# Modulation vectors on four column groups of 32 with 256-wide pieces instead of two of 64, and ten convolution taps moved into the attention heads

## What is computed

```python
def modulation(cvec, w_mod_l, b_mod_l):
    m = jax.nn.silu(cvec) @ w_mod_l + b_mod_l          # w_mod_l: 1024 x 6144
    return m.reshape(cvec.shape[0], 6, D_MODEL)

def trunk_layer(x, mod, ...):
    sh1, sc1, g1, sh2, sc2, g2 = [mod[:, i][:, None, :] for i in range(6)]
    h = rms_norm(x, n1) * (1.0 + sc1) + sh1
    q, k, v, u = jnp.split(h @ w_in, ...)
    # QK-norm; rotary positions for latent tokens
    attn = block_attention(q, k_all, v_all)            # 8 heads of 64, 2 key heads
    conv = conv_module(u, dw_w, dw_b, ln_g, ln_b)      # gate, 31 taps depthwise, layer norm, silu
    x = x + g1 * (jnp.concatenate([attn, conv], axis=-1) @ w_out)
    h2 = rms_norm(x, n2) * (1.0 + sc2) + sh2
    x = x + g2 * grouped_moe(h2, ...)                  # 16 experts, top 2 of one group
    return x, k, v
```

## Time and profile before

| | |
|---|---|
| median of 3 runs | 1130.35 us |
| all three | 1130.08, 1130.35, 1140.29 us |
| profiled execution | 1134.84 us, of which the span 1133.0 us |
| granted TensorE clock, mean | 0.938 of full |
| TensorE busy (products) | 1003.9 us, 89% |
| VectorE, ScalarE, GpSimd busy | 393.6, 152.3, 116.3 us |
| moved by DMA | 329.83 MB, mean 291 GB/s |

### The profile page before, as it was taken

How to read it: one execution, slowest core, us unless ns; L and a number is a source line. 1 busy time by engine, 2 the same in 40 slices (tenths; PEclk the granted TensorE clock), 3 DMA queues, 4 the chain that set the end, 5 groups by cost and what they waited for, 6 DMA issues and landing times. The chain is left out here.

```text
span 1133.0 us, 11425 instructions
## 1 busy us (share of the span) xinstructions
PE 1003.9 (89%) x4328; PEld 471.3 (42%) x4328; DVE 393.6 (35%) x857; ACT 152.3 (13%) x357; POOL 116.3 (10%) x176
## 2 busy tenths in 40 slices
PE   4799999999799998899899989999788888987993
PEld 1555544545233333333366534555433333333331
DVE  0159954334411111111035996434511111111106
ACT  1100144220000000000020014422000000000001
POOL 0100400501000000000111020050100000000001
PEclk9899989998899999999899999999689899999897
DMA  9926991259999996999980375235966999999814
GB/s 341 354 117 238 291 366 70 95 189 360 419 404 423 425 372 273 413 422 424 360 306 24 149 277 215 75 115 195 371 237 240 417 422 425 424 423 422 353 28 167
DMA packets 64406, 329.83 MB, mean 291 GB/s; under 512 B 6992, under 2 KB 9680, under 8 KB 47924
## 3 DMA queue, kind: packets, MB, share of 16 engines
q1 hardware_dynamic: 44224, 277.89, 61.2%
q0 software_dynamic: 8496, 28.68, 6.9%
q10 hardware_dynamic: 11588, 21.95, 5.9%
HBM read 306.67 MB, written 21.82 MB: 290 GB/s over the span
## 5 line engine op out<-in xcount | busy, mean ns | idle before, releaser
L1746 PE MATMUL ps<-big 128*64 128x512 f32 x1024 | 245.5, 631 | 29.0 <-DMA big<-in_w_up_dram 11.8
L1762 PE MATMUL ps<-big,scr 128*64 128x512 f32 x624 | 151.0, 623 | 5.3 <-DVE scr L1399 4.3
L1441 PE MATMUL ps<-big 128*128 128x384 f32 (+2 forms) x448 | 147.9, 492 | 5.2 <-ACT big L777 5.2
L1746 PEld LDWEIGHTS ps<-big 128*64 128x64 f32 x1024 | 81.7, 145 | 168.1 <-issue 157.1
L1102 DVE SCALAR_TENSOR_TENSOR scr<-scr,convw 128x384 f32<-128x384 f32 x240 | 134.0, 611 | 2.3
L1410 DVE TENSOR_TENSOR scr<-ps,scr 128x256 f32<-128x256 f32 x32 | 13.6, 425 | 315.5 <-ACT scr L932 315.5
L1441 PEld LDWEIGHTS ps<-big 128*128 128x128 f32 x448 | 86.0, 193 | 64.7 <-issue 24.6
L1457 PE MATMUL ps<-big,cs_rep 128*64 128x512 f32 x320 | 80.8, 656 | 14.0 <-DMA big<-in_w_mod_dram 14.0
L1762 PEld LDWEIGHTS ps<-big,scr 128*64 128x64 f32 x624 | 51.2, 143 | 91.1 <-issue 89.0
L1662 PE MATMUL ps<-big 128*128 128x512 f32 x192 | 84.4, 594 | 1.4 <-ACT big L817 1.4
L1746 PE MATMUL ps<-big,scr 128*64 128x512 f32 x224 | 51.3, 612 | 5.9 <-DVE scr L1388 5.9
(11 more groups left out here) (220 smaller groups left out, 819.7 us busy)
## 6 DMA issues: line engine op xcount, KB each, us to landing
big<-in_w_gate_dram SPq DMA_DIRECT2D x32, 2048.0 KB, 15.8
big<-in_w_up_dram SPq DMA_DIRECT2D x32, 2048.0 KB, 19.7
big<-in_w_down_dram SPq DMA_DIRECT2D x32, 2048.0 KB, 16.7
big<-in_w_mod_dram SPq DMA_DIRECT2D x23, 2048.0 KB, 15.5
big<-in_w_in_dram SPq DMA_DIRECT2D x6, 2048.0 KB, 26.8
expert_rows<-scr ACTq DMA_DIRECT2D x74, 128.0 KB, 8.2
big<-in_w_out_dram SPq DMA_DIRECT2D x4, 2048.0 KB, 15.6
expert_rows<-x ACTq DMA_DIRECT2D x1, 6912.0 KB, 42.0
```

The costliest lines, as they stand in the source:

```text
L1441: mm = pe.matmul(out, stationary(k), moving(k), start=(k == 0), stop=(k == n - 1))
L1746: mm = pe.matmul(ps[b * TT:(b + 1) * TT, bank, :].rearrange("p (m n) -> p m n", m=2), tokens(k), w[:, :, k, b * HF:(b + 1) * HF], start=(k ...
L1762: mm = pe.matmul(ps[b * TT:(b + 1) * TT, bank, :], src[:, k % 2 * P + k // 2 * TT:k % 2 * P + (k // 2 + 1) * TT], w[:, k, b * SEG:(b + 1) ...
```

## The change

`LANES` goes from 2 to 4. With it `LW` goes from 512 to 256 and `LP` from 64 to 32. A vector becomes 8 x 4 products of 32 x 256. The column products of a vector become 8 x 4 instead of 8 x 2, each with 32 columns of weights. `lane_in` and `lane_out` issue four DMAs instead of two each time, each over half the partitions (or the same two rows) and half as wide. `mod_take` handles 256 columns instead of 512. The expected semaphore counts follow. `rowC` is now the first 256 columns of `sg`. The tap constants go from 80, 6, 6, 4, 4 to 80, 6, 0, 0, 5: the 6 taps between rope(0) and rope(1) and the 4 behind mod_take(2) are taken away in each layer, and the heads take 26 instead of 16.

```diff
--- before.py
+++ after.py
@@ -34,7 +34,7 @@
 NT = CAP // TT
 HF = FF // 2
 SEG = 512
-LANES = 2
+LANES = 4
 LW = D // LANES
 LP = P // LANES
 SLOTS = 6
@@ -124,7 +124,7 @@
 for first_, n0, more_ in ((0, 16, 15), (1, 15, 16), (2, 16, 15)):
     CONV_ORDER += [p for n in range(more_) for p in ((first_, n0 + n), (first_ + 1, n))]
 CONV_ORDER += [(3, n) for n in range(15, TAPS)]
-EARLY_TAPS, ROPE_TAPS, BETWEEN_TAPS, LATE_TAPS, HEAD_TAPS = 80, 6, 6, 4, 4
+EARLY_TAPS, ROPE_TAPS, BETWEEN_TAPS, LATE_TAPS, HEAD_TAPS = 80, 6, 0, 0, 5
 assert sorted(CONV_ORDER) == [(m, n) for m in range(CM) for n in range(TAPS)]
 
 
@@ -286,12 +286,13 @@
         kT = cut(512)
         acc = cut(CM * CAP).rearrange("p (m n) -> p m n", m=CM)
         zT = cut(CM * CONV_W).rearrange("p (m n) -> p m n", m=CM)
-        assert o >= 5120 + 3 * LW
+        assert o >= 6656
 
         qk_sq = scr[:, TILES * 640 + 2 * 640:2 * TILES * 640 + 2 * 640].rearrange("p (t n) -> p t n", t=TILES)
         vall = cut(4 * KVW).rearrange("p (c n) -> p c n", c=4)
         ck = cut(KVW)
-        sg = rowC = cut(CH)
+        sg = cut(CH)
+        rowC = sg[:, 0:LW]
         assert o <= 9832
         hT_all = big[:, at_hT:at_hT + TILES * D].rearrange("p (j k n) -> p j k n", j=TILES, k=KD)
         gate_sig = [h[:, m, CH:CH + CAP] for m in range(3)] + [h[:, 2, 0:CAP]]
@@ -595,7 +596,7 @@
 
                 pool.wait_ge(mod_taken, taken_at(l, 2))
                 lane_out(pool, mod_dram[:, 2 * D:3 * D], rowC, modC_st)
-                pool.wait_ge(modC_st, (l + 1) * 32)
+                pool.wait_ge(modC_st, (l + 1) * LANES * 16)
                 spread(gateB[:, :, :], 2, bcG_in)
 
                 pool.wait_ge(slot_used[slot_of(("in", l, 3))], uses(("in", l, 3)))
@@ -626,7 +627,7 @@
                     if t:
                         ln_silu(t - 1)
                 ln_silu(2)
-                pool.wait_ge(modB_st, l * 48 + 48)
+                pool.wait_ge(modB_st, (l + 1) * (LANES + 1) * 16)
                 spread(scaleB[:, :, :], 4, bcA_in)
                 spread(shiftB[:, :, :], 3, bcA_in)
 
@@ -651,7 +652,7 @@
 
                 pool.wait_ge(mod_taken, taken_at(l, 5))
                 lane_out(pool, mod_dram[:, 5 * D:6 * D], rowG, modG_st)
-                pool.wait_ge(modG_st, (l + 1) * 32)
+                pool.wait_ge(modG_st, (l + 1) * LANES * 16)
                 spread(gateB[:, :, :], 5, bcG_in)
                 for e in range(E):
                     def run(t):
@@ -961,22 +962,22 @@
 
                 bank = mod_bank(l, c)
                 if c == 2:
-                    dve.wait_ge(rowC_in, (l + 1) * 32)
+                    dve.wait_ge(rowC_in, (l + 1) * LANES * 16)
                 if c == 3:
-                    dve.wait_ge(rowB_in, (l + 1) * 48)
+                    dve.wait_ge(rowB_in, (l + 1) * (LANES + 1) * 16)
                 if c == 5:
-                    dve.wait_ge(rowG_in, (l + 1) * 32)
+                    dve.wait_ge(rowG_in, (l + 1) * LANES * 16)
                 if c == 8:
                     dve.wait_ge(mod_half_ps, l + 1)
                 else:
                     n = pieces(l, min(c, 4 if c == 9 else c))[-1][0]
                     dve.wait_ge(slot_used[slot_of(n)], uses(n))
                 if c < 2:
-                    v.tensor_copy(rowA[:, c * LW:(c + 1) * LW], ps[:, bank, :]).then_inc(mod_taken, 1)
+                    v.tensor_copy(rowA[:, c * LW:(c + 1) * LW], ps[:, bank, 0:LW]).then_inc(mod_taken, 1)
                     return
                 if c < 8:
-                    row = (rowC[:, :], rowB, None, rowG)[c - 2]
-                    v.tensor_tensor(row, ps[:, bank, :], row, ALU.add).then_inc(mod_taken, 1)
+                    row = (rowC, rowB, None, rowG)[c - 2]
+                    v.tensor_tensor(row, ps[:, bank, 0:LW], row, ALU.add).then_inc(mod_taken, 1)
                 else:
                     half = slice(c % 2 * SEG, (c % 2 + 1) * SEG)
                     row, gain = rowS[:, half], gainB[:, half]
@@ -1454,7 +1455,7 @@
                             loaded(n)
                         w = slot_k(slot_of(n), b - a)[:, k - a, :]
                         for lane in range(LANES):
-                            mm = pe.matmul(ps[lane * LP:(lane + 1) * LP, mod_bank(l, j), :], cs_rep[:, k, :],
+                            mm = pe.matmul(ps[lane * LP:(lane + 1) * LP, mod_bank(l, j), 0:LW], cs_rep[:, k, :],
                                            w[:, lane * LW:(lane + 1) * LW], start=(k == 0), stop=(k == KD - 1))
                         if k == b - 1:
                             mm.then_inc(slot_used[slot_of(n)], 1)
```

## The result

The changed kernel takes 1125.53 us (median of 20 runs, 1119.47 to 1132.13), the kernel before, timed beside it, 1131.41 (20 runs, 1127.87 to 1140.29). The ratio is 0.9945, with a 95% interval of 0.9924 to 0.9966: 6 us faster, where 17.9 were forecast. 1125.53 is above the range's end of 1125. The profiled execution of the changed kernel has 1125.83 us, against 1134.84 of before.

A forecast was written before the change was run, and what follows sets the result against it. Outside the experts engine waits bind, inside them often the weights' stream. 4.0 + 4.2 + 3.3 + 0.7 + 4.6 + 2.7 - 1.6 = 17.9 us: profiled 1134.84 to 1117.0, median forecast 1112.5, range 1106 to 1125.

The forecast's parts named there:

- The pace: TensorE's vector rows: four column groups run side by side, 54 ns a record; column products 26 to 28 ns.
- Rivals 1 to 3: Records: (1) 59 to 65 ns, 1119.8 us, 10%; (2) two groups together, 1127, 8%; (3) groups in turn, 1175, 5%.
- Start and attention: Shorter vectors, copies and columns, and moved taps: gain 4.0 us at the start, 4.2 in layer 0's attention, 4.6 in layer 1's.
- The heads: Attention heads: the added taps hide in VectorE's idle time while TensorE runs without a gap; no change.
- rival 4: Pace comes, part given back through VectorE, GpSimd, the stream or lower clock in waits: 12 to 6 us left, 17%.
- Routing: Ahead of the experts: layer 0's expert 0 starts 5.7 us earlier, layer 1 gains 2.7; gather moves with slot_tok.
- The experts' stream: Layer 0's experts: weights for expert 4 land late, so only 3.3 of 5.7 us pass; in layer 1 all passes.
- The column products of layer 1: Alone on TensorE ahead of expert 15: 128 rows at 27 ns against 64 at 61, gain 0.7 us.
- The stores ahead of layer norm: Before the output projection, GpSimd issues two stores more: loss 0.8 us in each layer, 1.6 together.

The follow-up runs named there:

- dma_late: Changed kernel with GpSimd's four gate-bias issues moved behind the three rope roots; 1123.7 us, 0.9936.
- cols_split: Changed kernel with layer 1's column products in two places, vector 0's in another bank and one expert earlier; 1121.8 us, 0.9921.
- before_fill_more: Kernel before with unused extra products: 11 rounds before layer 1's last rope, 5 and 16 in the gather waits; 1126.31 us, 0.9947.
- fill_gather: Changed kernel with unused extra products in the two gather waits alone, 14 rounds in layer 0, 18 in layer 1; 1125.56 us, 0.9947.

## Why the prediction went wrong, by its own steps

**The pace (right).** 56 ns a row of the vectors and 18 of the column products, 54 and 27 forecast. Rivals 1 to 3 are out. So is the reading by which matmuls would be decoded at about 62 ns each, from TensorE: Matmul & The Clock Gate of the Trainium skill: four rows start within 20 ns and a fifth 216 ns behind the first, and column products take 18 ns a row, ends taken in, or 36 a product of two rows. The same page of the Trainium skill has a floor of about 25 ns from start to start: rows went under it here, whole products did not. Its three column groups at 2.38 times one are not met either; four ran at 54 ns, four times one.

**Start and attention (right).** Start: from vector (0,1)'s beginning to the projection 15.1 us before and 10.5 after, 4.6 gained where 4.0 stood. Layer 0: VectorE's second add follows the vectors' beginning by 13.7 us instead of 16.7, 3.0 gained where 4.2 stood. Most of the missing 1.2 is the last vector rows: 1.94 us at the lower level, 1.07 at the upper, behind a wait of 2.35 us, which the working had made possible and not counted. GpSimd's roots came late as said, if less: VectorE's first add stands 1.9 us earlier where 1.5 was reckoned, so that the roots cost 1.3 of the 3.25 us and not 1.8. VectorE's timeline after:

```profile
112.41 0.83 DVE L1121 TENSOR_TENSOR scr<-scr,stat 128x640 f32<-128x640 f32 x1 [0.83 <-POOL stat L585]
...
119.14 0.82 DVE L1121 TENSOR_TENSOR scr<-scr,stat 128x640 f32<-128x640 f32 x1 [0.83 <-POOL stat L585]
...
135.69 0.42 DVE L980 TENSOR_TENSOR big<-ps,big 128x256 f32<-128x256 f32 x1 [3.05 <-PE ps L1458]
```

Layer 1: 4.1 where 4.6 stood. Of the pair's gain at the start 2.9 us are neither: the transposes of x (L1495) begin at 25.1 us instead of 28.0 since the first loads landed earlier in that execution.

**The heads (a term put at nothing).** "So nothing" was argued from VectorE's cover and held at the upper level: heads are 6.68 us apart in all kernels. But the heads' length is set by the clock in their first 20 us, and that differs from one execution to the next; extra products in the wait ahead of them shorten the low stretch and don't make it sure to be gone. The working named this in rival 4, which it gave 17%, and counted the vectors' saving in layer 1 as worth nothing. Against the one profile of before the heads lost 2.4 us in layer 0 and 5.1 in layer 1 over three profiles; over all profiles, as said above, it is under 2 us that can be put down to the change.

**Routing (the gather taken as fixed).** Layer 0 should have won 4.9 us up to expert 0 and won 2.4 (2.5 in the pair). Up to the last router products 1.45 were lost, where 0.8 stood: the stores' 0.6, and router rows at the lower level (3.33 us for 16 instead of 1.96). slot_tok was 3.8 us earlier behind them, as forecast (4.05), and the rows behind the transposes saved 1.6 (1.7). But the gather gave 1.4 back, which no step had: the sum let it follow its issue at the old distance. Layer 1's 1.9 did not come at all: slot_tok gained 1.8 instead of 2.7, the gather took 9.3 us instead of 8.0 behind its issue, and TensorE's wait grew to 9.80, with the lower level through the products around it.

```profile
815.35 1.95 PE L1731 MATMUL ps<-table_sb,scr 128*128 128x128 f32 x8 [9.80 <-DMA scr<-h_rows,slot_tok]
```

**The experts' stream (nothing to take back).** The working let 2.4 us of layer 0's gain be lost to the stream of weights. Expert 4 starts 47.9 us behind expert 0 instead of 48.6, after a wait of 1.67 us for its up weights; what was to be given back had not been won.

**The column products of layer 1 (sign wrong).** 0.7 us of gain was priced by TensorE's own time, 4.0 to 2.2. The block with what follows takes 7.2 instead of 4.7: 2.5 lost there, though the stages of dma_late and cols_split show that it need not reach the end. The price of fetching 64 products more was in no row that I had taken; the 3.47 us of "issue" that the kernel before already had ahead of an expert at 457.94 was its sign, and I had passed over it:

```profile
457.94 8.78 PE L1746 MATMUL ps<-big 128*64 128x512 f32 x32 [3.47 <-issue]
```

**The stores ahead of layer norm.** TensorE waits 0.62 and 0.59 us for GpSimd there, 0.8 forecast each.

In sum, in us, three profiles against one: heads 7.5, the way to expert 0 2.5 in layer 0 and 1.9 in layer 1, experts with the column products 1.5, attention of layer 1 0.5, less 2.6 more gained at the start and in layer 0's attention: 11.3, which is what is missing. So three steps failed: the heads at nothing, the gather at its old length, and the column products priced without their instructions. The longer gather of layer 0 and the stall ahead of expert 15 are in every four-group trace whose edit leaves them alone. The 7.5 of the heads is mostly the one short profile of before. What stays open is the share of each in the medians: by the runs' clocks the lower level is 5 to 9 us (the estimate above), before_fill_more moved by 6 us where the clock had little to give, and the experts' stages differ by 5 us and more from one profile to the next in kernels that differ nowhere near them.

## What to carry to other kernels

A stage that hides behind another engine's wait is not free to shorten: ask what clock TensorE will have when the wait ends, and whether it can have work in it. Price a bundle of tiny products by its instructions too, by the "issue" waits that the profile already has near it. And when a transfer that is waited for moves in time, look up which packets it will run beside.

## What the runs showed of the hardware beyond that

Four groups of 32 columns run side by side at no loss in fp32, with each group's pace for its own columns (216 ns from one row of 256 to the group's next, where 64 columns and 512 took about 429). Column products on strided weights of 32 columns in four groups take 18 ns a row; every fourth starts about 62 ns behind the last fourth. Every wait of TensorE that the timeline calls "issue" and that is over 0.9 us long ended 1.2 to 2.0 us behind a 16 KB packet of the queue named instruction. Once the granted clock had fallen, it stayed at 0.51 for 20.5 us of work without a gap (671.8 to 692.3); in other executions of the same kernel it was up again after 7. And the level's mean over a kernel says little of its time: fill_gather's runs have 0.935, the changed kernel's 0.928, and both take the same time.
